# One pipeline for both attentions of a first mixer, with its last input columns and norms between, and one pipeline for a fourth mixer

## The reference, cut to what matters

```python
p = h @ w_in                      # q, k, v, o, gates, mq: 2568 columns
h = num / maximum(|den|, exp(-m)) # mLSTM: scores weighed by exp(gate sums), causal
hm = hm * rsqrt(mean(hm*hm) + EPS) * g_out      # norm by head
hm = sigmoid(o) * hm
mo = softmax(mq @ mk.T / 8) @ mv                # 4 heads of 64
mix = concat([hm, mo]) @ w_out
```

```python
sel = top_k(sum_h w_idx * relu(q_idx @ k_idx.T), 128)
logits = q @ k[sel] / sqrt(128) - slope[head] * distance
y = concat([softmax(logits) @ v[sel], softmax(qm @ mk.T) @ mv]) * silu(gate)
x = layer_norm(ALPHA * x + y @ w_out)
```

## Time and profile before

| | |
|---|---|
| time, median of 3 runs | 2278.38 us (2277.81 to 2281.79) |
| time of the profiled execution | 2280.4 us |
| its span, first to last instruction | 2278.9 us |
| PE busy | 2111.9 us, 93% |
| DVE busy | 1168.8 us, 51% |
| ACT busy | 883.9 us, 39% |
| mean granted PE clock | 0.958 |

### The profile page before, as it was taken

The page is one execution under the profiler, slowest core; times in us unless marked ns, Lnnn a source line. Parts: engine busy times, 40 slices in busy tenths (PEclk is TensorE's granted clock), DMA queues, the critical chain, the costliest instruction groups (busy, mean ns, idle before and its releaser), DMA issues.

```text
span 2278.9 us, 24588 instructions
## 1 busy us (share of the span) xinstructions
PE 2111.9 (93%) x9984; PEld 1716.7 (75%) x9984; DVE 1168.8 (51%) x2252; ACT 883.9 (39%) x1565; POOL 231.7 (10%) x155
## 2 busy tenths in 40 slices
PE   6998899999997999999999999999998899799787
PEld 6986688888786777788887878878776666577575
DVE  5325453333226666453332237998865248655553
ACT  5336443222124356442322222477451222456520
POOL 1000010000002000010000003766500000000000
PEclk9998599999998999999999999999999899999998
DMA  6330022233233212222222322322322312011211
GB/s 225 114 117 11 10 83 93 93 99 105 102 107 114 67 55 75 93 97 98 93 93 93 111 93 96 108 74 74 102 74 74 110 56 70 23 38 56 74 56 56
DMA packets 28800, 192.60 MB, mean 85 GB/s; under 512 B 3264, under 2 KB 3408, under 8 KB 7440
## 3 DMA queue, kind: packets, MB, share of 16 engines
q1 hardware_dynamic: 24848, 175.96, 22.5%
q0 software_dynamic: 3264, 12.99, 1.7%
q10 hardware_dynamic: 576, 2.10, 0.2%
HBM read 186.84 MB, written 4.19 MB: 84 GB/s over the span
## 4 chain that ended last, share of the span: by engine, by line
PE 77%; DVE 15%; ACT 6%; issue 1%; DMA 0%; POOL 0%; SPq 0%; DVEq 0%; POOLq 0%; ACTq 0%
PE bank L390 22%; PE bank L391 21%; PE bank L392 21%; DVE bank L1971 4%; PE bank L1660 2%; DVE WL L362 1%; PE bank L1551 1%; ACT WH L348 1%; PE bank L1090 1%; PE bank L1648 1%; PE bank L1099 1%; PE bank L1027 1%; PE bank L1561 1%; PE bank L2112 1%; PE bank L1653 1%
## 5 line engine op out<-in xcount | busy, mean ns | idle before, releaser
L390 PE MATMUL bank<-XH,WH 128*128 128x512 f32 (+1 forms) x1504 | 598.5, 398 | 25.4 <-DVE XL L551 10.3
L392 PE MATMUL bank<-XH,WL 128*128 128x512 f32 (+1 forms) x1504 | 568.5, 378 | 0.0
L391 PE MATMUL bank<-XL,WH 128*128 128x512 f32 (+1 forms) x1504 | 567.9, 378 | 0.0
L362 DVE TENSOR_TENSOR WL<-RAW,WH 128x2048 fp32r<-128x2048 f32 x128 | 293.2, 2291 | 462.8 <-ACT WH L348 462.8
L348 ACT ACTIVATE WH<-RAW 128x2048 fp32r<-128x2048 f32 x148 | 282.3, 1908 | 347.1 <-PE bank L392 341.7
L390 PEld LDWEIGHTS bank<-XH,WH 128*128 128x128 f32 x1504 | 286.8, 191 | 94.6 <-issue 24.7
L391 PEld LDWEIGHTS bank<-XL,WH 128*128 128x128 f32 x1504 | 287.1, 191 | 54.4 <-issue 5.6
L392 PEld LDWEIGHTS bank<-XH,WL 128*128 128x128 f32 x1504 | 286.3, 190 | 53.3 <-issue 0.6
L1971 DVE SCALAR_TENSOR_TENSOR bank<-conv_in,cols,bank 128x512 f32<-128x512 f32 x290 | 198.1, 747 | 1.1
L390 PE MATMUL bank<-WH,XH 128*128 128x512 f32 (+2 forms) x416 | 154.6, 372 | 9.8 <-DVE XL L551 6.3
L391 PE MATMUL bank<-WL,XH 128*128 128x512 f32 (+2 forms) x416 | 153.7, 369 | 0.0
(11 more groups left out here) (316 smaller groups left out, 3023.8 us busy)
## 6 DMA issues: line engine op xcount, KB each, us to landing
RAW<-weights SPq DMA_DIRECT2D x164, 1024.0 KB, 4.9
row_a<-rows POOLq DMA_DIRECT2D x7, 512.0 KB, 5.8
row_b<-rows POOLq DMA_DIRECT2D x6, 512.0 KB, 6.0
x_res<-x SPq DMA_DIRECT2D x1, 2048.0 KB, 16.7
kv<-mem_park POOLq DMA_DIRECT2D x2, 1024.0 KB, 5.1
out<-x_res ACTq DMA_DIRECT2D x4, 512.0 KB, 2.6
mem_tok<-mem SPq DMA_DIRECT2D x1, 1024.0 KB, 5.0
mem_tok<-mem POOLq DMA_DIRECT2D x1, 1024.0 KB, 8.4
```

Source lines behind the costliest of these rows:

```text
L362: dve.tensor_tensor(WL[j][:, :], RAW[j][:, :], WH[j][:, :].bitcast(F32), ALU.subtract).then_inc(*lo.mark())
L390: pe.matmul(ps, ah, bh, start=first, stop=False)
L391: pe.matmul(ps, ah, bl, start=False, stop=False)
L392: return pe.matmul(ps, al, bh, start=False, stop=last)
```

## The change

In the first mixer the input columns stand in another order: gates, q and k, mq, o, v. The sums, turns and rows move between the column groups (after the third group, after half of the fourth and after the whole). The o gate's sigmoid moves before the jobs. Of the sixth group, which holds values of heads 1 to 3, tile 0 comes before the jobs and tiles 1 to 3 come between them, one piece of three products in each of the first 24 steps. All 32 jobs, mLSTM and memory, form one pipeline by tiles, on a ring of six banks, with delays of 0, 2, 3 and 4 steps. Each head is squared when it is done. When a tile's jobs are done its norm, gate and turn follow, and the first two units of `w_out` are split in quarters. The first products with `w_out` run in an order that leaves tile 3 last. Score buffers, `c_row` and `diag` get places of their own, so that the parts of `x` in XH and XL can stay.

In the fourth mixer six gate units move into the choice of keys, two query units stay beside its last tile, and four query units move beside the jobs. The stage beside tile 3 so has four units in place of two. The 64 jobs form one pipeline, woven with six units, of which the last two are gates. DVE adds distance and mask a job ahead.

```diff
-    order += ... run("b_mem_q", 2) + run("b_q", 6)
-    return order + run("b_gate", 8) + run(("b_out", 0), 4) + run(("b_out", 1), 4)
+    order += ... run("b_mem_q", 2)
+    order += run("b_gate", 6) + run("b_q", 6) + [("b_gate", 6), ("b_gate", 7)]
+    return order + run(("b_out", 0), 4) + run(("b_out", 1), 4)
...
     def in_a_pe():
...
+        in_a_unit_pe(0, 1)
+        for i in range(1, 3):
+            for b in range(2):
+                in_a_unit_pe(i, b)
+        log_sums_pe()
+        in_a_unit_pe(3, 0)
+        proj_turn_pe()
+        in_a_unit_pe(3, 1)
+        c_rows_pe()
+        for b in range(2):
+            in_a_unit_pe(4, b)
...
+    FIRST_JOBS = [(kind, 4 * t + h) for t in range(NT) for kind, h in
+                  (("lstm", 0), ("lstm", 1), ("mem", 0), ("lstm", 2), ("mem", 1), ("lstm", 3), ("mem", 2), ("mem", 3))]
+    FIRST_ORDER = staggered(len(FIRST_JOBS), (0, 2, 3, 4))
+    PER_TILE = 2 * LH
+    NORM_STEP, TURN_STEP = PER_TILE + 3, PER_TILE + 4
...
+    def last_columns_pe(t, b, q):
+        u, kb = U["in_a", 2 * LAST + b], 4 * b + q
+        if kb == 0:
+            PE.wait_ge("split_lo", u + 2)
+            take_bank("beside", "in_a", LAST, t)
...
+    LAST_COLUMNS = [(t, b, q) for t in range(1, NT) for b in range(2) for q in range(4)]
+    QUARTERS_FROM = len(LAST_COLUMNS) + 1
+
+    def mlstm_pe():
+        for b in range(2):
+            for q in range(4):
+                last_columns_pe(0, b, q)
...
+        for n, step in enumerate(FIRST_ORDER):
+            other = LAST_COLUMNS[n:n + 1]
+            for stream, k in woven(len(step), len(other)):
...
+            if n >= TURN_STEP and (n - TURN_STEP) % PER_TILE == 0:
+                turn_mixed_tile_pe((n - TURN_STEP) // PER_TILE, "six")
+        turn_mixed_tile_pe(NT - 1, "six")
...
     def mlstm_dve():
...
+            if QUARTERS_FROM < n <= QUARTERS_FROM + 8:
+                lower_quarter_dve((n - 1 - QUARTERS_FROM) % 4)
+            if n >= NORM_STEP and (n - NORM_STEP) % PER_TILE == 0:
+                head_norm_dve((n - NORM_STEP) // PER_TILE)
+            if n >= TURN_STEP and (n - TURN_STEP) % PER_TILE == 0:
+                parts_of_tile_dve(("mixed", 0), (n - TURN_STEP) // PER_TILE)
...
+    LATE_TILE = [(0, 0), (1, 0), (2, 0), (0, 1), (1, 1), (3, 0), (2, 1), (3, 1)]
...
+    def select_units(t):
+        if t == 0:
+            return [("b_mem_q", i) for i in range(2)]
+        return [("b_gate", 2 * (t - 1) + i) for i in range(2)] + ([("b_q", 0), ("b_q", 1)] if t == NT - 1 else [])
...
+    B_JOBS = job_steps(64)
+    BESIDE_JOBS = [("b_q", i) for i in range(2, 6)] + [("b_gate", 6), ("b_gate", 7)]
+    B_ORDER = woven(FEATURE_STEPS * len(BESIDE_JOBS), len(B_JOBS))
...
     def gate_b_pe():
-        for event in (("sel", NT - 1), ("kv2", 1), ("emptied", U["b_gate", 0] - 1, 1)):
+        for event in (("sel", NT - 1), ("kv2", 1), ("emptied", U["b_mem_q", 1], 1)):
...
+        for s, k in B_ORDER:
...
+            for stage, j in B_JOBS[k]:
+                if stage == 0 and "head" in jobs[j]:
+                    i, c = divmod(jobs[j]["head"], 2)
+                    PE.wait_ge(*after("emptied", U["b_q", i], c))
+                job_pe(stage, "dsa", j, jobs[j])
...
     def gate_b_dve():
+        jobs = sparse_jobs()
+        job_bias_dve("dsa", 0, jobs[0])
...
+                job_dve(stage, "dsa", j, jobs[j])
+                if stage == 0 and j + 1 < len(jobs):
+                    job_bias_dve("dsa", j + 1, jobs[j + 1])
```

More of the change, by code:

```diff
@@ L921, in build @@
[L921 to L931, removed]
@@ L933, in T_of, with in_a_out_act, in_a_tile_act @@
-    def T_of(i, w):
-        return T_buf[i % 4][:, 0:w]
+        in_a_unit_pe(0, 1)
[9 more added lines that the diff above has]
+            in_a_unit_pe(4, b)
+    def in_a_out_act(i):
+        for t in range(NT):
+            in_a_tile_act(i, t)
+    def in_a_tile_act(i, t):
+        ACT.wait_ge(*after("full", "in_a", i, t))
+        act.activation(proj[:, t, i * A_CHUNK:(i + 1) * A_CHUNK], bank_of("in_a", i, t)[:, 0:A_CHUNK], AF.Copy).then_inc(
+            *A.mark("emptied", "in_a", i, t))
@@ new lines, in in_a_act @@
+    def in_a_act():
+        for i in range(LAST):
+            split_act()
+            if i == 3:
+                proj_turn_act()
+            in_a_out_act(i)
+            split_act()
+            if i == 0:
+                lstm_gates_act()
+            elif i == 3:
+                c_rows_act()
+        for t in range(NT):
+            o = proj[:, t, COL_O:COL_O + 768]
+            ACT.wait_ge(*after("emptied", "in_a", LAST - 1, t))
+            act.activation(o, o, AF.Sigmoid).then_inc(*A.mark("o_gate", t))
@@ L936, in proj_turn_pe @@
+    def in_a_dve():
+        for i in range(LAST):
+            lower_dve()
+            if i == 3:
+                lstm_sums_dve()
+            lower_dve()
+            if i == 0:
+                gate_sum_dve()
     def proj_turn_pe():
+        for t in range(NT):
+            PE.wait_ge(*after("emptied", "in_a", 2, t))
         for h in range(2 * LH):
@@ L1051, in lstm_dve @@
-    def lstm_dve():
+                    ACT.wait_ge(*after("full", "lstm_out", j))
+                    ACT.wait_ge(*after("lstm_recip", j))
+                    act.activation(mixed[:, t, h * LV:(h + 1) * LV], bank_of("lstm_out", j)[:, 0:LV], AF.Copy,
+                                   scale=stat(4, i)).then_inc(*A.mark("emptied", "lstm_out", j))
+                    head_square_act(j)
+            if n and LAST_COLUMNS[n - 1:n] and LAST_COLUMNS[n - 1][1:] == (1, 3):
+                in_a_tile_act(LAST, LAST_COLUMNS[n - 1][0])
@@ L1059, in lstm_dve @@
                     if i >= 4:
-                        DVE.wait_ge(*after("full", "lstm_out", i - 4))
+                        DVE.wait_ge(*after("full", *turned(i - 4)[1]))
                     dve.tensor_tensor_reduce(T_of(i, w), c_row[:, h, 0:w], const[:, K_CAUS + 512 - w:K_CAUS + 512], 1.0,
@@ L1695, in job_dve @@
             else:
-                if i >= job["rings"][0]:
-                    DVE.wait_ge(*after("full", "turn", name, i - job["rings"][0]))
-                dist, slope, chosen = job["bias"]
-                dve.scalar_tensor_tensor(out=S, in0=dist, scalar=slope, in1=chosen, op0=ALU.mult, op1=ALU.add).then_inc(*V.mark())
-                DVE.wait_ge(*V.so_far())
+                DVE.wait_ge(*after("bias", name, i))
                 dve.tensor_tensor_reduce(S, bank_of(name, i)[:, 0:w], S, ATT_SCALE, NEG, ALU.add, ALU.max,
@@ L1711, in job_dve, with job_bias_dve @@
                 dve.tensor_scalar(S, S, stat(4, i), None, ALU.mult).then_inc(*V.mark("divided", name, i))
+    def job_bias_dve(name, i, job):
+        if job["bias"] is not None:
+            if i >= job["rings"][0]:
+                DVE.wait_ge(*after("full", "turn", name, i - job["rings"][0]))
+            dist, slope, chosen = job["bias"]
+            dve.scalar_tensor_tensor(out=job["S"][:, 0:job["width"]], in0=dist, scalar=slope, in1=chosen, op0=ALU.mult,
+                                     op1=ALU.add).then_inc(*V.mark("bias", name, i))
     def mem2_job(i):
         return second_memory_job(0, i // 4, i % 4, S_mem, T_mem, i)
-    GATE_STEPS = 2 * FEATURE_STEPS
     def gated_dve(name, p):
```

397 lines of the change are left out of this document (205 added, 192 removed).

## The result

The changed kernel takes 2245.35 us (median of four runs, 2242.63 to 2246.93), the kernel before 2278.14 on the same chip: a ratio of 0.9864, 95% interval 0.9848 to 0.9880. That is 32.8 us less where 55 were forecast, and 22 us above the predicted 2223.4. The range ended at 2246; 0.9864 of the 2278.4 that it was made against is 2247.4. The profiled execution took 2242.63 us, with a span of 2241.2; PE is busy for 2093.4 us (93%) at a mean clock of 0.970. Of all executions behind this document two ran far slower than the rest, one of 2403.74 us in `side_spread_units` and one of 3118.51 us in `side_again`, at mean clocks of 0.835 and 0.629; they stand in no ratio.

What follows compares the result with a forecast made beforehand. PE, busy 93% of the span, was taken as the bound. 21.3 us less in the first mixer and 33.7 in the fourth, together 55.0, took the median 2278.4 to 2223.4 us; range 2208 to 2246.

Steps and rivals of the forecast that it cites:

- Part 1: First mixer: sums, turns and rows between column groups, 13.1 us. Fourth mixer: choice gets four units, 43.5 us, PE never waits.
- Parts 2, 3 and 5: First mixer: idle before the last columns, 4.7 us; eight pieces of tile 0, 6.2; the end up to `w_out`, 4.4.
- Part 4: First mixer: pipeline of 32 jobs, 83 us. Fourth mixer: bias computed a job ahead, 0 booked beyond 1.7 us.
- +2.5 each, 5 in all: First mixer's pipeline: delay from norms of tiles 0 and 1 on DVE's queue and the six-bank ring, 2.5 us each.
- PE's sum of 71.6: First mixer's pipeline: PE's own work on mLSTM jobs, memory jobs, pieces and turned tiles, 71.6 us.
- small hand-overs: First mixer's pipeline: filling, draining and other hand-overs, +4 us.
- rival B: First mixer's pipeline: hand-overs, ring and norms add half a us more in each of 36 steps, +18 us, 2241; chance 0.15.
- Rival A: First mixer's pipeline: the last tile's jobs, without filler, fall to half clock, +15.8 us, 2239; chance 0.14.
- D: First mixer: the whole merged pipeline runs at 1.2 GHz, +65 us, 2288, slower than before; chance 0.04.
- 72 for 83 and 155 for 162: Lower bounds: first mixer's pipeline 72 us (PE alone), fourth mixer's jobs 155 (all clock regained, no stall); total given as 2209.
- Part 2: Fourth mixer's jobs: PE's 186.1 us lose two units (21.8) and 6 of lost clock, leaving 158.3 us.
- Part 3: Fourth mixer's jobs: one pipeline drains once, leaving 3.7 us of waits; ACT's table loads fall from 16 to 4.

Runs made afterwards that it cites:

- side_spread_units: Changed kernel with turned tiles in side banks, norm in two steps, and first pieces waiting only for their own half of the weights: 2233.93 us, ratio 0.981.
- side_again: Changed kernel with turned tiles in the side banks, timed again on one chip with the unchanged changed kernel: 2233.02 to 2252.68 us, profiled execution 2252.68.
- sums_first: Changed kernel with DVE's log sums and diagonals ahead of the low part of the seventh weight unit: 2243.76 us, ratio 0.986.
- side_spread: Both cures: changed kernel with turned tiles' halves in free banks of the last columns and each norm in two steps: 2242.8 us, ratio 0.985.
- side: Side banks alone: changed kernel with halves of turned tiles 0 to 2 in free banks of the last columns, not the ring: 2232.7 us, ratio 0.980.
- best: Changed kernel with side banks, sums ahead of the low part, first pieces waiting only for their own weights half, norm in one piece: 2233.21 us, ratio 0.981.
- before_again: The kernel before, unchanged, profiled once more: 2273.99 us.
- fourth_only: The kernel before with only the fourth mixer's part of the change: 2245.66 us, ratio 0.986.
- delay_2: `best` with two useless 128x512 products on PE just ahead of the first product with `w_out`: 2227.05 us, ratio 0.977.

## Why the prediction was wrong

From the forecast for a like execution, 2225.4 us, to the profiled 2242.6 it is 17.2 us: 12.1 from the first mixer, 5.0 from the stages between, 1.8 from the fourth mixer (334.2 to 302.3 is 31.9, not 33.7), and 1.6 back behind it. The other 4.8 of 22 is that before's profiled execution lies 2.0 us above its median and the changed kernel's 2.7 below its own.

**First mixer.**
- Part 1 (13.1 us): 15.0. The turns waited 3.16 us for the bank of the log sums, which DVE copied late. `sums_first` shows that this wait alone is worth under 1 us, since ACT's evictions follow.
- Parts 2, 3 and 5 held. Of the idle 4.7 us, 2.4 could be filled with pieces.
- **Part 4 failed, in the term "+2.5 each, 5 in all" for norms and ring** and in the clock, for whose loss it booked nothing. I counted norm and ring as separate small delays. They are one: norm and parts hold up DVE's product, and the turned tile's two banks bring forward the moment at which PE needs it. The three stops come to 8.1 us, with half clock behind each. The 10.5 us over 83 are 5.1 of idle time (16.5 where 11.4 stood) and 5.4 of PE time (76.95 where 71.6 stood). The side banks alone give 7.9 of them back (85.6). PE's sum of 71.6 was sound: with both cures, at a clock of 1.00, it is 70.4. The small hand-overs were booked too low: 13.2 us are idle there though the stops are gone, where 11.2 stood with norms and ring and 6.2 without. So that the jobs then take 83.6 us, near the forecast's 83, doesn't bear the forecast out. It is rival B's mechanism, banks that come free late, but at three places and not in each step. Rival A and D did not come: no tile stayed at half clock.
- A slip in the sum of the bounds: 72 for 83 and 155 for 162 take 18 us off 2223.4, which is 2205 and not 2209. It doesn't touch the upper end, which was the one passed.

The rule of the Trainium skill, "TensorE: Matmul & The Clock Gate", section "A second HAM failure mode: psum-queue depth-cycling", that I set against this term has the clock swing between both levels when PE idles briefly and often while it cycles through PSUM banks. The trace agrees more than I allowed: after the first stop the mean is about 0.9, and 1.00 stood there in my forecast. Most of it came with the stops of 2.3 us and more, not with the cycling as such: the first tile cycles through the ring at 1.00, and so does the whole stretch in `side_spread`. Yet `side` and `best`, with no wait over 1.53 us in the jobs, stand at 0.96, so the stops are not all of it.

**What the gain was measured against.** The deeper error is in the base. I took the memory jobs' 0.54 as a property of the kernel, and weighed only whether the new one would share it. It is one of two states of one and the same program. Up to `w_out` the changed kernel is 9.2 us ahead of one state (277.57) and 1.8 us behind the other (266.53). `before_again` and `fourth_only` told them apart; from one profile they can't be.

**Between the stages** I booked nothing. The 11.0 us that before's better state has at `w_out` are 6.5 at the last choice (1819.88 less 1813.36), and the changed kernel's 9.2 are 4.25: in both, short waits fall into half clock that the first profile escaped. The kernel before alone shows that no instruction there is guilty: it has both sets of values. In `delay_2` all three have the values of the first profile, with `w_out` 1.7 us later than in `best`. What sets the outcome is left open; it may go with when the wait comes, but the time of `w_out` alone doesn't decide it: `side` and `side_again`, the same program with `w_out` 0.4 us apart, ended 24 us apart in the sliding mixer. The Trainium skill, "TensorE: Matmul & The Clock Gate", Part 1, calls the number of slow matmuls at a kernel's start run-variable, by the phase of the clock gate. No run here tests that start; what they show in mid-kernel is also variable from run to run, at 1.3 to 24 us, and whether it has the same cause is open.

**Fourth mixer: 31.9 us, forecast 33.7, right for reasons that were half wrong.**
- Part 1 held: the 9.7 idle us are filled, DVE was not late.
- Part 2 held in its number: PE's busy time falls from 186.4 (counted up to 2154.1 us) to 155.7, which is 21.8 for two units and 8.9 of clock (6 booked). But without the bias ahead it is 161.9, 2.7 of clock.
- **Part 4 failed.** "Beyond the 1.7 just named I book 0": the bias ahead is worth 15.7 us in the changed kernel and 11.3 in the old rounds (334.3 to 323.0). Idle time went from 17.7 to 8.3 us, and lost clock by 6.3. That it does so by shortening the chain of scores, maximum and exponential, at many small places, is my reading.
- **Part 3 failed as well, the other way.** One pipeline and the moved units without it bring 16.3 us (334.3 to 318.0), not 33: 17.7 us stay idle, where 3.7 stood. The two errors cancel. Four table loads came, as forecast, but no wait of 3 us behind Td near the end: the longest in the jobs is 1.97. The table loads explain 1.43 us of a long wait and not most of it.

## What to carry to other kernels

Profile the kernel before more than once, or look at its runs' clocks, before you book the return of lost clock as a gain: a stretch at half clock may be a state that many executions don't have (two of five profiles here). A helper block that takes banks from a ring shifts the ring for all others; look at which engine must release the bank that is now needed, and what stands ahead of that release on its queue. Take each ingredient of a change out by itself, even when the sum came right.

## What the hardware showed unexpectedly

- The same instructions without gaps hold either clock level: the memory jobs for 38 us (step 1.44 or 2.62 us), the sliding mixer's first jobs for about 50 us (168.7 or 144.6 us for the stage).
- A short wait of 2.24 us costs 1.6 us more in one execution and nothing in another, and with 1.7 us of useless work ahead the last choice of keys came 2.6 us earlier than in `best`, in one profile of each.
- Waits of up to 1.53 us left the clock of a pipeline at 1.00 over 83.6 us in `side_spread` and at 0.96 over some 85 us in `side` and `best`.
- Where the clock held, times repeat closely: the fourth mixer's choice and jobs took 302.20 to 302.38 us in twelve profiles of its new form.
